# VectorE's order in a step of dilated attention: the subtraction ahead of the later step's maxima

## The reference, cut to what matters

```python
for window, dil in ((128, 1), (512, 4), (2048, 16)):
    ...
    s = jnp.einsum('bnirhe,bnjrhe->bnrhij', qs, kk) * scale
    s = jnp.where(valid[None, :, None, None], s, -jnp.inf)
    mx = jnp.max(s, axis=-1, keepdims=True)
    p = jnp.exp(s - mx)
    den = jnp.sum(p, axis=-1)
    o = jnp.einsum('bnrhij,bnjrhe->bnirhe', p, vv) / jnp.moveaxis(den, -1, 2)[..., None]
    lse = jnp.moveaxis(mx[..., 0] + jnp.log(den), -1, 2)
```

## Time and profile before

| | |
|---|---|
| median of 3 runs | 3830.38 (3827.08 to 3835.16) |
| the profiled execution's own time | 3839.2 |
| its span in the trace | 3837.6 |
| the phase's steps 0 to 107, with maxima | 1114.32 to 1388.24 |
| its steps 108 to 143, without maxima | 1388.24 to the end of the phase's work, about 1457.9 |
| TensorE busy, share of the whole span | 90% |
| mean granted TensorE clock, share of full speed | 0.929 |

### The profile page before, as it was taken

The page is one execution under the profiler, slowest core; times in us unless marked ns, Lnnn a source line. Parts: engine busy times, 40 slices in busy tenths (PEclk is TensorE's granted clock), DMA queues, the critical chain, the costliest instruction groups (busy, mean ns, idle before and its releaser), DMA issues. The chain is left out here.

```text
span 3837.6 us, 61229 instructions
## 1 busy us (share of the span) xinstructions
PE 3464.3 (90%) x21989; PEld 2976.2 (78%) x21989; DVE 2049.5 (53%) x4128; ACT 1561.5 (41%) x3047; POOL 737.3 (19%) x1044
## 2 busy tenths in 40 slices
PE   8999999899958896678997995999989999999996
PEld 8999999444436664545665784999989999899996
DVE  2211100589946555744665446565675656756564
ACT  3321111688823433322444224444455434554342
POOL 0111100467712334422442001000010000200000
PEclk9999999899958786688999997999999999999998
DMA  6564443210054316576996553434444344432222
GB/s 206 204 208 153 155 148 125 86 42 9 9 124 87 80 34 166 153 207 206 358 355 210 168 175 116 139 123 138 139 141 157 116 153 135 139 108 67 69 75 77
DMA packets 444516, 533.48 MB, mean 139 GB/s; under 512 B 94885, under 2 KB 382246, under 8 KB 439238
## 3 DMA queue, kind: packets, MB, share of 16 engines
q1 hardware_dynamic: 415584, 410.59, 35.0%
q0 software_dynamic: 20992, 66.08, 5.2%
q10 hardware_dynamic: 7656, 53.04, 4.1%
HBM read 435.82 MB, written 143.91 MB: 151 GB/s over the span
## 5 line engine op out<-in xcount | busy, mean ns | idle before, releaser
L3453 PE MATMUL p_DP<-p_UH,p_WH 128*128 128x352 f32 x1536 | 497.6, 324 | 21.2 <-issue 14.4
L3454 PE MATMUL p_DP<-p_UL,p_WH 128*128 128x352 f32 x1536 | 496.6, 323 | 0.0
L3455 PE MATMUL p_DP<-p_UH,p_WL 128*128 128x352 f32 x1536 | 496.3, 323 | 0.0
L3453 PE MATMUL p_UP<-p_TH,p_WH 128*128 128x352 f32 x1344 | 438.8, 327 | 53.8 <-DVE p_TL L3363 36.9
L3454 PE MATMUL p_UP<-p_TL,p_WH 128*128 128x352 f32 x1344 | 433.6, 323 | 0.0
L3455 PE MATMUL p_UP<-p_TH,p_WL 128*128 128x352 f32 x1344 | 433.6, 323 | 0.0
L408 PE MATMUL p_PP<-p_WH,p_HH 128*128 128x384 f32 (+1 forms) x1224 | 416.6, 340 | 8.4 <-DVE p_HL L342 4.4
L409 PE MATMUL p_PP<-p_WL,p_HH 128*128 128x384 f32 (+1 forms) x1224 | 407.0, 332 | 0.0
L410 PE MATMUL p_PP<-p_WH,p_HL 128*128 128x384 f32 (+1 forms) x1224 | 406.7, 332 | 0.0
L3453 PEld LDWEIGHTS p_DP<-p_UH,p_WH 128*128 128x128 f32 x1536 | 290.7, 189 | 23.4 <-issue 21.3
L321 ACT ACTIVATE p_PT<-p_PP,p_rs 128x384 f32<-128x384 f32 (+1 forms) x153 | 87.3, 571 | 530.1 <-PE p_PP L410 530.1
(11 more groups left out here) (454 smaller groups left out, 6833.4 us busy)
## 6 DMA issues: line engine op xcount, KB each, us to landing
p_WU<-in_w_up SPq DMA_DIRECT2D x48, 1024.0 KB, 5.4
p_WD<-in_w_down SPq DMA_DIRECT2D x192, 256.0 KB, 2.9
cw_K<-in_cache_sb_k SPq DMA_DIRECT2D x192, 192.0 KB, 4.2
cw_V<-in_cache_sb_v POOLq DMA_DIRECT2D x192, 192.0 KB, 5.1
out_s_wk<-in_cache_win_k ACTq DMA_DIRECT2D x64, 382.5 KB, 3.5
out_s_wv<-in_cache_win_v ACTq DMA_DIRECT2D x64, 382.5 KB, 4.1
p_HH<-scratch_xh SPq DMA_DIRECT2D x34, 512.0 KB, 4.6
p_HL<-scratch_xl SPq DMA_DIRECT2D x34, 512.0 KB, 5.3
```

The costliest lines, as they stand in the source:

```text
L3453: pe.matmul(out, hi, rhi, start=first, stop=False, skip_group_check=True)
L3454: pe.matmul(out, hi, rlo, start=False, stop=False, skip_group_check=True)
L3455: return pe.matmul(out, lo, rhi, start=False, stop=last, skip_group_check=True)
```

## The change

In VectorE's loop over the steps the two calls change places. No instruction is added or removed, no semaphore and no buffer changes, and the other engines' code is the same. The maxima ahead of step 0 and the steps from 108 on are as before.

```diff
             for j in range(TOTAL):
+                shifted(j)
                 if j + LEAD < TOTAL:
                     maximum(j + LEAD)
-                shifted(j)
                 h, i = divmod(j, CY)
                 if i == CY - (LEAD - CY) and h + 1 < HB:
                     joint(h + 1)
```

## The result

| | before | after |
|---|---|---|
| median | 3828.66 (3822.03 to 3835.16, 6 runs) | 3789.95 (3785.09 to 3796.56, 6 runs) |
| ratio, 95% interval | | 0.9905 (0.9893 to 0.9917) |
| span of the profiled execution | 3837.6 | 3783.5 |
| steps 0 to 107 in it | 273.92 | 235.20 |

The changed kernel takes 38.7 us less by the medians and 36.4 by the ratio (32 to 41); 3791 was forecast. The two profiled executions differ by 54.1 us, but only 38.7 of this (273.92 - 235.20) lie in the steps with maxima. The rest lies in the other phases, which the change doesn't touch: over the traces of all fourteen kernels in this document, the time outside these steps varies from 3547 to 3564 us.

What follows compares the result with a forecast made beforehand. A ring of waits bounded the loop, TensorE having least slack. A head falls from 61.4 to 51.9 + 0.8 = 52.7 us; 8.7 over 4.5 heads is 39, and 3830.4 - 39 = 3791 us, range 3772 to 3814.

Steps and rivals of the forecast that it cites:

- the ring: Steps with maxima: scores, natural, maxima and subtraction wait in turn, period 2.40 us at k = 2; subtraction held 0.98.
- the steps with total: VectorE at k = 0, 2, 4, 22: total delays the next subtraction, about 0.8 us a head in all.
- k = 8 to 10: Steps of a head where TensorE has gaps of 0.5 us each between values and the next scores.
- The sum: 24 steps of a head go from 61.4 to 51.9 + 0.8 = 52.7 us; 39 us over 108 steps.
- the signs named in the prediction: Expected in the trace: heads of 51 to 54 us, TensorE idle below 2, joint 0 to 2 us behind `MR`.
- I count nothing for it here: Readback of the maxima before joint: about 4.0 us slack, 3.2 us of gaps removed, so no cost.
- they gain nothing: Steps k = 5, 6, 7, 11, 15 and 19: no TensorE gap, values long at the lower clock, so no gain.
- TensorE's clock rises: Rival, chance 0.20: all steps with maxima at the upper clock, 49.2 us a head, 55 us gained, 3775.
- The clock didn't fall: Rival, chance 0.05: TensorE at 1.2 GHz in all steps with maxima, 21 us slower, 3851.
- Half the gain: Rival, chance 0.16: second ring, handing over or ScalarE keeps steps apart; 20 us gained, 3810.
- ScalarE's backlog: ScalarE at k = 7 to 11, busy near 2.4 us a step, might keep steps apart; new step near 2.5.
- the order doesn't matter: Rival, chance 0.06: another wait fully replaces the subtraction's 0.98 us lateness, so no change, 3830.

Runs made afterwards that it cites:

- the other execution: Joint moved from k = 12 to k = 16 in the kernel before, old order kept: 3827.43 against 3826.3, ratio 1.0005; its trace has a 267.5 us stretch.
- a late joint: New order with joint moved from k = 12 to k = 16, against the kernel before: 3773.43 against 3826.3, ratio 0.9868.

## Why the prediction was right, and where its steps were not

**The bound, and what the order frees: right.** The maxima stood in the ring and held up a subtraction that was ready. The forecast of single steps was near: k = 0, 2, 4 and 22, the steps with total, were put at 2.2, 2.2, 1.9 and 2.3 and came out at 2.18, 2.18, 1.91 and 2.27; k = 8 to 10 were to lose 0.5 each and lost 0.5 each. For these three the reason is another than the forecast's: with the long values TensorE alone needs 2.48 (so in the run with the new order in k = 5 to 11), with short ones the turns of scores and subtraction need the same 2.48. The steps from 108 on stayed at 65.3.

**The sum: the right number by luck, from two errors that cancel.** A head was put at 52.7, and the mean of heads 2 to 4 is 52.6. But it holds neither the durations nor the idle time of the forecast. Two of the signs named in the prediction failed: TensorE's idle time was to be below 2 us a head and is 2.9 to 4.9, and joint, which was to come 0 to 2 us behind `MR`, stood for it, which the prediction had called a sign of being wrong.

*"I count nothing for it here"*, of the readback, failed. joint stood 2.3 to 3.6 us in the first four heads, 11.8 in all, and the steps behind it ran at the lower clock. Moving joint, or the writes ahead of the loads of V, is worth 14 to 15 us by the ratios (0.9868 and 0.9866 against 0.9905). In the third head the account closes. From the first load of V to joint passed 26.4 us before, of which 3.5 were slack, with the 1.7 us that the readback takes from issue to landing in place of the 1.4 taken for it. After, the same way was 5.4 us shorter, not 3.2, because k = 5 to 7 and 11, which had no gaps, got shorter too (2.6 together in the table by k), and the readback was issued 22.7 us behind the load instead of 21.2. That is 3.4 us too late, and joint stood 3.5.

*"they gain nothing"*, of k = 5 to 7, failed for the reason behind it: the durations were taken at the lower level of the clock, and the new order lifted it. k = 5 and 6 fell from 2.03 to 1.50. In all TensorE's busy time fell by 17.5 us between the two traces (8.9 against the other execution), and idle time by 21.3 (23.5) where the forecast had about 38.

**The rival "TensorE's clock rises"** had the mechanism right, both parts of it: a higher level, and then joint against the readback. Its size was off. It gave a head 49.2 with 2.7 us of waiting. The waiting was 2.4 to 3.6 in heads 2 to 4, and it brings the lower level back for k = 13 to 15, which the rival left out. Without the wait it gave 46.5 a head, and 47.7 was measured with a late joint. The steps k = 8 to 10 are enough to explain this: the rival took 0.5 off each of them for the clock, and there, as the rows above show for k = 9, the turns of scores and subtraction leave nothing more to save. That is 1.5 a head.

With a late joint the granted clock was 1.00 in the second and third head, after each of the four stalls values were long, and in the run with k = 5 to 11 alone TensorE, busy 18.05 of 18.05 us by its records, stood at 0.54. The Trainium skill, "TensorE: Matmul & The Clock Gate", section "What's actually happening", says that the default is the throttled clock and that activity releases it. The 1.00 and the long values behind the stalls agree with that; the 0.54 does not follow from it.

**The other rivals.** The clock didn't fall on the whole. Half the gain would have needed dearer handing over; it stayed at 0.05 in the rows of k = 6 (scores end at 1230.85, the subtraction starts at 1230.90). ScalarE's backlog didn't keep the steps apart: k = 8 to 10 take 2.48 by scores and subtraction alone, and TensorE's waits for masked weights come to 2.5 us in all 108 steps. That the order doesn't matter is refuted.

**A misreading without weight.** Of TensorE's slices in the earlier trace rows only one near the loop reads below 8, the 5 from about 1055 to 1151 us, and it holds only the first steps; the next low digits (6, 6, 7) begin at 1439, behind the loop. Most of the loop lies in slices of 8, 8 and 9. Where it stands was known from the earlier trace rows, and no number rests on the slices.

## What to carry to other kernels

Where one engine's in-order queue holds work of two ages, put first the work that another engine's next step waits for, and behind it the work that has a whole period's time. To price it, don't add up the engine's work: ask for each instruction on which side of the wait that closes the ring it stands. The same instruction, 0.34 us in each of 108 steps, cost nothing that could be measured on one side and 35 us on the other.

When a loop gets faster, every fixed latency that it covered becomes a candidate: write down each transfer's slack and the saving ahead of it, at both clock levels. Durations of TensorE taken from a loop with gaps may belong to a clock that the loop without them won't have.

## What the runs showed of the hardware

The level of TensorE's clock in seven steps was set neither by these steps alone nor by the five ahead of them alone: from the second head on they ran at 0.50 before, at 0.55 to 0.73 and at 0.54 to 0.63 with one of the two closed up, and at 0.78 to 1.00 with both. Idle times of 1.60 to 3.06 us were each followed by values of 1.98 to 2.07 in place of 1.13.

The strided scores of dilation 16 take 0.80 to 0.81 and those of dilation 4 (full width) 1.28 to 1.29, whether the values beside them are long or short. So a stretch can be gapless at the lower level by its records and get shorter at the upper one only by its values.
